# Storing the expert weights of a hybrid encoder with interleaved rows, so that the 16 parts of a transfer read neighbouring rows of device memory

## The reference

```
def swiglu(t, w1, w3, w2):
    return (jax.nn.silu(t @ w1) * (t @ w3)) @ w2

def moe_swiglu(x, router, w1, w3, w2):
    ...
    logits = (t @ router).astype(jnp.float32)
    top_val, top_idx = lax.top_k(logits, TOP_K)
    probs = jax.nn.softmax(top_val, axis=-1)
    combine = jnp.sum(jax.nn.one_hot(top_idx, N_EXPERTS, dtype=jnp.float32) * probs[..., None], axis=1)
    out = jnp.zeros((bsz * seq, d), jnp.float32)
    for e in range(N_EXPERTS):
        out = out + combine[:, e:e + 1] * swiglu(t, w1[e], w3[e], w2[e])
```

## Time and profile before

| | |
|---|---|
| time, median of 3 runs | 1901.42 us (1899.17 to 1902.48) |
| span of the profiled execution (first to last instruction) | 1891.2 us |
| median of the runs less that span | 10.2 us |
| PE busy over the span | 1811.4 us, 96% |
| bytes moved by DMA | 473.02 MB, mean 250 GB/s |

### The profile page before, as it was taken

The page is one execution under the profiler, slowest core; times in us unless marked ns, Lnnn a source line. Parts: engine busy times, 40 slices in busy tenths (PEclk is TensorE's granted clock), DMA queues, the critical chain, the costliest instruction groups (busy, mean ns, idle before and its releaser), DMA issues.

```text
span 1891.2 us, 63618 instructions
## 1 busy us (share of the span) xinstructions
PE 1811.4 (96%) x29088; PEld 1605.7 (85%) x29088; DVE 767.7 (41%) x1790; ACT 332.1 (18%) x786; POOL 102.6 (5%) x44
## 2 busy tenths in 40 slices
PE   7998988999999999898899999999999999999997
PEld 6877877577776787787749999999999999999996
DVE  7987645202111498664523222222322222222224
ACT  3243412102000424342211000000000000000000
POOL 4600000001000340000000000000000000000000
PEclk9999999999999999999999999999999999999999
DMA  7323212523434333222375999999999999999992
GB/s 292 131 90 112 90 54 105 211 95 139 166 137 169 115 102 111 90 90 69 112 277 229 416 399 409 412 401 404 402 414 402 411 407 402 410 401 407 409 407 106
DMA packets 55080, 473.02 MB, mean 250 GB/s; under 512 B 5264, under 2 KB 5552, under 8 KB 20944
## 3 DMA queue, kind: packets, MB, share of 16 engines
q1 hardware_dynamic: 37744, 292.04, 39.7%
q10 hardware_dynamic: 16880, 177.18, 23.1%
q0 software_dynamic: 368, 2.64, 0.4%
HBM read 470.77 MB, written 1.06 MB: 249 GB/s over the span
## 4 chain that ended last, share of the span: by engine, by line
PE 82%; DVE 11%; issue 3%; ACT 2%; DMA 1%; SPq 0%; DVEq 0%; ACTq 0%
PE bank L1053 29%; PE bank L977 14%; PE bank L813 8%; PE bank L865 8%; PE bank L887 4%; PE bank L485 3%; PE bank L845 3%; PE bank L827 2%; PE bank L645 2%; PE bank L1004 1%; PE bank L1043 1%; DVE arena L1731 1%; DMA ring<-in_w_in 1%; PE bank L596 1%; DVE arena L1736 1%
## 5 line engine op out<-in xcount | busy, mean ns | idle before, releaser
L1053 PE MATMUL bank<-arena,ring 128*64 128x88 f32 x8192 | 333.0, 239 | 0.0
L1053 PEld LDWEIGHTS bank<-arena,ring 128*64 128x64 f32 x8192 | 319.9, 137 | 0.0
L1979 DVE TENSOR_TENSOR arena<-arena,bank 128x88 f32<-128x88 f32 x224 | 55.0, 246 | 544.0 <-ACT arena L1330 543.9
L1053 PE MATMUL bank<-arena 128*64 128x88 f32 x6144 | 245.2, 239 | 1.1 <-DVE arena L2022 1.1
L1053 PEld LDWEIGHTS bank<-arena 128*64 128x64 f32 x6144 | 236.9, 137 | 2.1 <-issue 1.4
L813 PE MATMUL bank<-xT,ring 128*128 128x256 f32 x1024 | 227.7, 381 | 0.0
L1330 ACT ACTIVATE arena<-bank 128x88 f32<-128x88 f32 (+1 forms) x246 | 63.4, 258 | 931.3 <-PE bank L1053 737.6
L813 PEld LDWEIGHTS bank<-xT,ring 128*128 128x128 f32 x1024 | 192.9, 190 | 30.4 <-issue 4.7
L977 PE MATMUL bank<-arena,ring 128*64 128x88 f32 x4096 | 178.0, 239 | 0.2 <-issue 0.2
L977 PEld LDWEIGHTS bank<-arena,ring 128*64 128x64 f32 x4096 | 167.1, 137 | 4.9 <-issue 0.5
L485 PE MATMUL bank<-xT,ring 128*128 128x256 f32 x736 | 164.9, 386 | 3.4 <-DMA ring<-in_w_in 2.5
(11 more groups left out here) (400 smaller groups left out, 1586.9 us busy)
## 6 DMA issues: line engine op xcount, KB each, us to landing
ring<-in_moe SPq DMA_DIRECT2D x66, 1536.0 KB, 9.6
ring<-in_moe ACTq DMA_DIRECT2D x62, 1536.0 KB, 10.1
arena<-in_moe SPq DMA_DIRECT2D x49, 1536.0 KB, 9.8
arena<-in_moe ACTq DMA_DIRECT2D x47, 1536.0 KB, 9.4
ring<-in_ffn SPq DMA_DIRECT2D x22, 1536.0 KB, 6.3
ring<-in_w_gate SPq DMA_DIRECT2D x32, 1024.0 KB, 5.0
ring<-in_w_in SPq DMA_DIRECT2D x14, 1536.0 KB, 6.5
ring<-in_w_branch SPq DMA_DIRECT2D x8, 1024.0 KB, 4.9
```

What stands on the lines that cost most here:

```text
L1053: last = mm(bank[c:c + STRIP, g * CAP:(g + 1) * CAP], w[:, at:at + STRIP], rhs[:, kt, :], start=(kt == 0), stop=(kt == KT - 1), skip_group ...
L1979: tt_(ACTIVE_H[:, i, :], ff_sl[:, s % 2, 0:CAP], bank[:, CAP:2 * CAP], ALU.mult)\
```

## The change

Inside each unit the host stores the 128 rows in another order. Stored row 16 i + q holds what was row 8 q + i (q from 0 to 15, i from 0 to 7). The kernel reads the unit through a view of three dimensions, q, i and column, so that every row still lands on its old partition. What was 16 groups of 8 consecutive rows, with 8 x 12,288 = 98,304 bytes from the start of one group to the start of the next, becomes 16 groups of 8 rows each of which lies 16 rows from the one before, and the starts of the groups are 12,288 bytes apart.

```
+        moe = A["moe"].rearrange("e s (i q) c -> e s q i c", q=16)
...
-                                act.dma_start(ex_slot[u % EX_RING], A["moe"][e + u // EX_STEPS, u % EX_STEPS])\
+                                act.dma_start(ex_slot[u % EX_RING], moe[e + u // EX_STEPS, u % EX_STEPS])\
                                     .then_inc(ex_loaded[u % EX_RING][0], 16)
...
-                sp.dma_start(ex_slot[s], A["moe"][0, s]).then_inc(ex_loaded[s][0], 16)
+                sp.dma_start(ex_slot[s], moe[0, s]).then_inc(ex_loaded[s][0], 16)
...
-                            expert_unit(steps, s, A["moe"][e + s // EX_STEPS, s % EX_STEPS])
+                            expert_unit(steps, s, moe[e + s // EX_STEPS, s % EX_STEPS])
...
-                        expert_unit(ps * (NE * EX_STEPS), s, A["moe"][0, s])
+                        expert_unit(ps * (NE * EX_STEPS), s, moe[0, s])
...
-    out["moe"] = np.stack([mlp(a["moe_w1"][0, e], a["moe_w3"][0, e], a["moe_w2"][0, e]) for e in range(NE)])
+    rows = np.arange(P).reshape(16, P // 16).T.reshape(-1)
+    out["moe"] = np.stack([mlp(a["moe_w1"][0, e], a["moe_w3"][0, e], a["moe_w2"][0, e])[:, rows] for e in range(NE)])
```

## The result

The changed kernel is slower by a fifth: 2332.6 us median of 4 runs (2293.9 to 2349.9) against 1900.6 us before (1899.2 to 1902.5), ratio 1.215 with a 95% interval of 1.206 to 1.223. The ratio rests on the two faster runs (2293.9 and 2324.7 us), and with all four it would be 1.227. I had forecast no change. The profiled execution took 2293.9 us with a span of 2291.6 us, 400.4 us more than the span before.

What follows compares the result with a forecast made beforehand. The prediction took PE to bound the expert stage, with loads landing about 8 us early. All terms were 0 on a span of 1891.2 us, plus 10.2 us outside it: 1901.4 us, range 1897.5 to 1906.

Steps and rivals of the forecast that it cites:

- What bounds the kernel before: Expert stage: PE sets the pace, 108.49 us per expert; the 406 GB/s is its demand, no memory limit.
- The time to spare, and the price of a slower load: Expert loads: 8 us to spare, spent once; 217 loads slower than 3.875 us each cost the rest, deciding at 400 GB/s.
- the stock: Expert loads: 8 us taken to lie between a load's landing and its use.
- item 3 of the change: Rate of an expert load: assumed to stay above 406 GB/s, so a term of 0.
- The slower rival: Expert loads: neighbouring rows crowd one part of memory; at 390 GB/s 26 us more, 1928 us; chance 0.11.
- Theory A: Expert loads: neighbouring rows crowd one part of the device memory, the mechanism of the slower rival (1928 us, chance 0.11).
- My far end: Expert loads: if they no longer overlapped, 6.2 us each, the stage would grow by 497 us, to 2398 us.
- the change doesn't do what it says: Expert loads: engines may not get consecutive groups of 8, so spreads are only exchanged; 1901 us; shares 0.85 with the forecast.
- A longer issue: Issue of expert loads on SP or ACT: even three times as long, 0.7 us more, covered by 8 us; term 0.
- The ceiling of the rate that I weighed: DMA peak rate: 435.2 GB/s for 16 ports against 433 seen, so less than 1% to win.

Runs made afterwards that it cites:

- f2: The changed kernel with interleave and outermost view size 32 in place of 16, timed in rounds against the kernel before: 1900.1 us against 1898.8 us, ratio 1.0007.
- e2: Against the kernel before, each unit stored as 4 pieces of 768 columns by 128 rows, read with 128 rows outermost: 1907.6 us against 1899.2 us.
- e1: The changed kernel's view with 16 outermost, but rows back at almost their old addresses, groups 102,400 bytes apart: 2412.7 us against 1899.2 us for the kernel before.
- e7: The changed kernel with 32 in place of 16 in row order and view: 1895.1 us against 1897.8 us for the kernel before.
- e3: Transfers alone from one queue, without the encoder, in nine stages varying row order, distances and partitions written: 822.7 us in all.
- e6: Half of the change: even units interleaved with the new view, odd units as in the kernel before: 2430.5 us.
- g1: The far-groups kernel (16 outermost, rows at almost their old addresses) timed again in rounds against the kernel before: 2353.7 us median of 4, ratio 1.243.
- f1: The changed kernel with every expert unit issued by SP and none by ACT: 2415.6 us.

## Why the prediction was wrong

- **What bounds the kernel before: right.** PE set the pace and asked for 406 GB/s. The interleave by 32 (f2) shows that a change in the order of reading is worth nothing as long as that rate is delivered. Nothing ran faster than the kernel before, as forecast.
- **The time to spare, and the price of a slower load: right in form.** The sum was 217 x (time of a unit - 3.875) - 8, deciding at 400 GB/s. After, the loads from 1012.8 us (the first issue by ACT) to about 2245 us take 5.68 us each. Put in, this gives 384 us, 2285 us in all, and the profiled execution took 2293.9. The 5.68 us are the length of the stage divided by its loads, so the agreement shows that the loads account for the loss, and is no test of their price. In e2, at 402 GB/s, the sum gives 0.2 us and PE waited for `in_moe` for 4.6 us. Landings there grew from 9.7 to between 17.1 and 18.5 us (medians by group), so the stock exists and was used up. Put into the sum, the 4.6 us make it about 4 us where I took 8.
- **The step that failed is item 3 of the change, "I take a rate that stays above 406 GB/s".** I bounded it only by the distance between rows in device memory, because that was what the change is described by. The measured rate is 255 to 309 GB/s in the slices of the stage, 5.68 us for a unit in place of 3.875. The rate fell because the new view has 16 as its outermost size, and this, by the inference below, alters which engine writes which partitions. e1 has that view and not the distances, and is slow. e7 and f2 have the distances and not the 16, and are not.
- **The slower rival had the right sign and a chance of 0.11, and the wrong mechanism.** Theory A doesn't survive e1, e3 and e7. Its price of 26 us also took a tenth off the peak, where pairs at one port can take off half. My far end, 2398 us for loads that don't overlap, lies beyond the result, but that is luck: the loads do overlap, and more than before (five in flight for 2.5). I put it aside with "the number in flight is not changed", which is true of the slots alone and has no bearing on a rate.
- **The rival "the change doesn't do what it says" named the place and drew the wrong end from it.** I wrote that the deal of the 128 rows to 16 engines isn't visible, and went on that an exchange of one spread for another moves little. The shape of the transfer was in front of me: 128 x 3072 before, 128 x 1 x 3072 from a source of 16 x 8 x 3072 after. A longer issue I had considered, and it was indeed 0.54 for 0.33 us at no cost. The deal I had not priced. The description ahead of the prediction took the old transfer for 16 groups of 8 consecutive rows, one for each engine. By the inference below an engine had two groups of 4 there, and it was the change that gave it 8 consecutive partitions.
- **The ceiling of the rate that I weighed** was beside the point. What mattered was the port map in the Trainium skill, "SBUF — State Buffer", section "Door 1: The DMA port swizzle". Engines that meet in pairs at its ports would leave half of 427 GB/s, which is an estimate, and 214 to 219 GB/s is what the transfers alone show from one queue.

What is shown: the loss follows the outermost size of the view and the partitions that a transfer writes, and not addresses, dimensions or issue time. With the same source and different partitions it is there or not (431 against 204 GB/s). What is inferred: that engines meet at ports, that an outermost 16 gives an engine 8 consecutive partitions, while an outermost 32, 64 or 128 gives it two groups of 4 on one port. No record of the trace names the engine of a packet.

## What to carry to other kernels

Look at the outermost size of a transfer's source: it seems to decide how the transfer is dealt to the DMA engines. For the 128 partitions of this kernel, keep that size at 32, 64 or 128, and don't load halves such as partitions 0 to 63. Both 16 outermost and halves gave half the rate from one queue alone (219 and 214 for 427 GB/s) and 242 to 309 GB/s from two queues in the encoder. The halves had a plain source. When a layout is changed, first compare the shape of the transfers, and ask which engine writes which partitions, before thinking about device memory. Don't read the DMA share as distance from the limit: the length of a packet (460 ns before, 540 to 900 ns for most packets of the stage after) or the GB/s of a window at full share tells it.

## What the runs showed of the hardware that was not expected

- Transfers of different kinds disturb each other. With the bad split on one unit in seven, each such unit costs 6.5 us, nearly three times what its own bytes would (2.3 us). Half the units cost at least as much as all of them (2430 us in e6, 2294 to 2350 us after, 2320 to 2413 us in e1 and g1).
- With the bad split the rate isn't fixed. Alone it is 219 GB/s from one queue and 247 to 264 from two, and in the encoder 222 to 309 (f1, e1 and the change). It drifts within a run (309 falling to 256 after, 222 rising to 276 in f1). Executions of the change then differ by 2.4% (2293.9 to 2349.9 us), where 17 of the kernel before lie within 0.6% (1894.0 to 1905.3 us).
- Pieces of 3,072 bytes run at 402 GB/s against 427 for 12,288 bytes, in the encoder and alone.
